# Two-layer diffusion trunk with a 32-expert layer: routed tokens moved by indirect DMA, experts ordered by count, plain float32 products

## The reference, cut to what matters

```python
def moe(h, lp):
    shp = h.shape
    t = h.reshape(-1, shp[-1])
    s = jax.nn.sigmoid((t @ lp['w_router']).astype(F32))
    _, idx = lax.top_k(s + lp['b_router'].astype(F32), TOP_K)
    s_sel = jnp.take_along_axis(s, idx, axis=-1)
    wts = s_sel / jnp.sum(s_sel, axis=-1, keepdims=True) * ROUTED_SCALE
    gates = jnp.sum(jax.nn.one_hot(idx, N_EXPERTS, dtype=F32) * wts[..., None], axis=1).astype(t.dtype)
    hid = jax.nn.silu(jnp.einsum('td,edf->tef', t, lp['w_exp1'])) * jnp.einsum('td,edf->tef', t, lp['w_exp3'])
    routed = jnp.einsum('tef,efd->td', hid * gates[:, :, None], lp['w_exp2'])
    shared = (jax.nn.silu(t @ lp['w_sh1']) * (t @ lp['w_sh3'])) @ lp['w_sh2']
    return (routed + shared).reshape(shp)
...
    h = rmsnorm(x, lp['g_norm2']) * (1 + sc2) + sh2
    x = x + g2 * moe(h, lp)
```

## Time and profile before

| | |
|---|---|
| three runs | 2008.7, 2008.95, 2011.85 us; median 2008.95 us |
| the profiled execution | 2008.79 us |
| its span, first to last instruction | 2007.3 us |
| around the span | 1.5 us |
| TensorE busy | 1676.0 us, 83% of the span |
| VectorE, ScalarE, GpSimd busy | 1128.2, 613.9, 677.4 us |
| moved by DMA | 315 MB, 157 GB/s over the span |

### The profile page before, as it was taken

How to read it: one execution, slowest core, us unless ns; L and a number is a source line. 1 busy time by engine, 2 the same in 40 slices (tenths; PEclk the granted TensorE clock), 3 DMA queues, 4 the chain that set the end, 5 groups by cost and what they waited for, 6 DMA issues and landing times. The chain is left out here.

```text
span 2007.3 us, 22880 instructions
## 1 busy us (share of the span) xinstructions
PE 1676.0 (83%) x7904; PEld 1209.8 (60%) x7904; DVE 1128.2 (56%) x1430; ACT 613.9 (31%) x1194; POOL 677.4 (34%) x293
## 2 busy tenths in 40 slices
PE   1344999988899999999985999978889999999994
PEld 0003445564777777777774444564777777777773
DVE  0112333373577777777775242372677777777775
ACT  0002122422243344333431112331443343334331
POOL 2202030031354454444543030030344454445442
PEclk9766999979899999999997899979989999999998
DMA  9994221202165565556651431110265565556551
GB/s 335 389 366 151 99 94 43 84 11 69 49 231 182 186 230 190 182 181 204 209 184 47 161 133 45 43 52 3 84 224 182 202 210 187 188 188 227 182 183 67
DMA packets 196679, 314.98 MB, mean 157 GB/s; under 512 B 18184, under 2 KB 153864, under 8 KB 193544
## 3 DMA queue, kind: packets, MB, share of 16 engines
q1 hardware_dynamic: 190792, 303.26, 43.9%
q0 software_dynamic: 5696, 10.77, 1.8%
q10 hardware_dynamic: 128, 0.13, 0.0%
HBM read 310.19 MB, written 5.94 MB: 157 GB/s over the span
## 5 line engine op out<-in xcount | busy, mean ns | idle before, releaser
L1547 POOL TENSOR_TENSOR low<-raw,high 128x2048 fp32r<-128x2048 f32 x64 | 421.3, 6583 | 522.8 <-DVE high L99 522.8
L1776 DVE TENSOR_TENSOR low<-raw,high 128x2048 fp32r<-128x2048 f32 x128 | 340.4, 2660 | 37.4 <-ACT high L1594 35.3
L749 PE MATMUL PS<-ringA,hT 128*128 128x512 f32 x672 | 302.8, 608 | 1.5 <-PE PS L749 0.6
L1664 PE MATMUL PS<-high,hTe 128*128 128x512 f32 x512 | 209.2, 409 | 69.1 <-POOL low L1547 64.2
L749 PEld LDWEIGHTS PS<-ringA,hT 128*128 128x128 f32 x672 | 128.2, 194 | 164.0 <-issue 161.6
L1665 PE MATMUL PS<-low,hTe 128*128 128x512 f32 x512 | 201.8, 394 | 0.0
L1666 PE MATMUL PS<-high,hTe 128*128 128x512 f32 x512 | 201.7, 394 | 0.0
L1580 ACT ACTIVATE hTe<-PS 128x512 fp32r<-128x512 f32 x256 | 153.4, 599 | 55.3 <-PE PS L1647 50.2
L99 DVE CAST high<-raw 128x2048 fp32r<-128x2048 f32 x128 | 156.3, 1221 | 17.4 <-DMA raw<-in_w_exp 16.6
L1722 PE MATMUL PS<-yh,PTb 128*128 128x512 f32 x384 | 153.7, 400 | 11.1 <-DVE acc L1809 11.1
L1664 PEld LDWEIGHTS PS<-high,hTe 128*128 128x128 f32 x512 | 96.6, 189 | 108.6 <-POOL low L1547 74.5
(11 more groups left out here) (292 smaller groups left out, 2645.8 us busy)
## 6 DMA issues: line engine op xcount, KB each, us to landing
raw<-in_w_exp SPq DMA_DIRECT2D x256, 512.0 KB, 4.8
raw<-in_w_exp SPq DMA_DIRECT2D x64, 1024.0 KB, 5.9
raw<-in_w_ada SPq DMA_DIRECT2D x24, 2048.0 KB, 26.8
ringA<-in_w_in SPq DMA_DIRECT2D x28, 1024.0 KB, 5.0
ringA<-in_w_out SPq DMA_DIRECT2D x8, 1024.0 KB, 4.9
ringB<-in_w_sh SPq DMA_DIRECT2D x8, 512.0 KB, 5.7
na_bias<-in_na_rpb POOLq DMA_DIRECT2D x32, 64.0 KB, 23.8
gate<-mod_rows POOLq DMA_DIRECT2D x4, 512.0 KB, 7.3
```

Of the source, the lines that this page charges most:

```text
L749: mm = pe.matmul(PS[:, u % 2, :], hT[:, k, t * P:(t + 1) * P], ring[:, s, c * 512:(c + 1) * 512], start=(k == 0), stop=(k == 7))
L1547: pool.tensor_tensor(hi(low[:, 1, :]), raw[:, 1, :], high[:, 1, :], ALU.subtract).then_inc(S["low_p"], 1)
L1664: pe.matmul(out, hi(ah), hi(wh), start=first, stop=False)
L1776: dve.tensor_tensor(hi(low[:, k, :]), raw[:, k, :], high[:, k, :], ALU.subtract).then_inc(S["low_v"], 1)
```

## The change

**Layout.** The host packs each expert's `w_exp1` and `w_exp3` beside each other, partition by partition, and `w_exp2` behind them: 16 KB and then 8 KB per partition in one row (`in_w_exp`, `in_w_sh`). One transfer brings up's weights (2 MiB), one brings down's (1 MiB).

**Units.** After the router the experts are ranked by count on the chip: experts 0 and 1 keep ranks 0 and 1 (their weights are loaded already in section B), the others follow by falling count. Ranks 0 to 9 get a unit of 128 slots each; the 22 other experts share 11 units, two experts of 64 slots side by side in column tiles (0, 0) and (0, 64). That makes 21 units, whole and paired ones alternating after the first two. A further pass over all units runs where a count exceeds its capacity.

```diff
+NS, NDF = 2, 8
+NF = NS + NDF
+NPAIR = (NE - NF) // 2
+NR13, NR2, NXG = 4, 5, 2
```

```diff
-                    norm_ev_dve(dve, 1, hT)
...
+                    dve.wait_ge(loaded, 64)
                     for t in range(T):
...
+                        dve.wait_ge(S["rstd_ready"], t + 1)
+                        v(dve.scalar_tensor_tensor(h2[:, t, :], x[:, t, :], rstd[:, t:t + 1], mrow[:, min(t, 1), 0, :], ALU.mult, ALU.mult))
+                        dve.tensor_tensor(h2[:, t, :], h2[:, t, :], mrow[:, min(t, 1), 1, :], ALU.add).then_inc(S["h2_ready"], 1)
```

```diff
+                    turn(0)
+                    pe.wait_ge(landed[3], 16)
+                    down(0)
+                    table(0)
+                    table(1)
                     turn(1)
+                    table(2).then_inc(S["table_mm"], 1)
+                    down(1)
                     turn(2)
                     down(2)
```

**Section C** is written out for the 21 units, with no cuts, no one-hot fetch and no one-hot return:

```diff
-                            pe.matmul(out, hi(ah), hi(wh), start=first, stop=False)
-                            pe.matmul(out, hi(ah), hi(wl), start=False, stop=False)
-                            return pe.matmul(out, hi(al), hi(wh), start=False, stop=last)
...
+                        for ranks in RANKS_OF[NS:]:
+                            expert = [sp.value_load(order[0:1, r:r + 1], min_val=0, max_val=NE - 1) for r in ranks]
+                            for r, e in zip(ranks, expert):
+                                i = place_of[r]
+                                if i >= NR13:
+                                    sp.wait_ge(S["w13_used"], i - NR13 + 1)
+                                sp.dma_start(ring13[:, i % NR13, :], A["w_exp"][l, e, :, W13]).then_inc(w13_in[i % NR13], 16)
...
+                                sp.dma_start(ring2[:, i % NR2, :], A["w_exp"][l, e, :, W2]).then_inc(w2_in[i % NR2], 16)
...
+                        def gather(u):
+                            b = u % NXG
+                            if u >= NXG:
+                                pool.wait_ge(xg_in[b], 16 * (u // NXG))
+                                pool.wait_ge(S["x_turned"], u - NXG + 1)
+                            pool.indirect_dma_start(xg[:, b, :], None, h2d[:, :], bass.IndirectOffsetOnAxis(ap=idx[:, 0, 0, u:u + 1], axis=0),
+                                                    bounds_check=T * P - 1, oob_is_err=False).then_inc(xg_in[b], 16)
...
+                        def scatter(u):
+                            b = u % 2
+                            if u >= 2:
+                                pool.wait_ge(y_out[b], 16 * (u // 2))
+                            pool.wait_ge(S["y_ready"], u + 1)
+                            pool.indirect_dma_start(yd[:, :], bass.IndirectOffsetOnAxis(ap=idx[:, 0, 1, u:u + 1], axis=0), y[:, b, :], None,
+                                                    bounds_check=T * P * TOPK - 1, oob_is_err=False).then_inc(y_out[b], 16)
...
+                        for u in range(NXG):
+                            gather(u)
+                        for u in range(NU):
+                            if u + NXG < NU:
+                                gather(u + NXG)
+                            scatter(u)
...
+                        def up(u):
+                            ranks = RANKS_OF[u]
...
+                            pe.wait_ge(S["xT_ready"], u + 1)
...
+                            for k in range(KC):
+                                for j, r in enumerate(ranks):
+                                    at, tile = columns(ranks, j)
+                                    mm = pe.matmul(PS[at, u % 2, :], xT[:, u % 2, k, at], w13_of(r, k),
+                                                   start=(k == 0), stop=(k == KC - 1), tile_position=tile)
+                            mm.then_inc(S["up_mm"], 1)
+                            if ranks[0] >= NS:
+                                pe.wait_ge(S["up_mm"], u + 1)
+                                pe.sem_inc(S["w13_used"], len(ranks))
...
+                        turn_in(0)
+                        for u in range(NU):
+                            up(u)
+                            if u + 1 < NU:
+                                turn_in(u + 1)
+                            if u:
+                                down(u - 1)
+                            turn(u)
+                        down(NU - 1)
...
+                        def keep(u):
+                            dve.wait_ge(S["down_mm"], u + 1)
...
+                            if u >= 2:
+                                dve.wait_ge(y_out[u % 2], 16 * (u // 2))
+                            dve.tensor_copy(y[:, u % 2, :].rearrange("p (b n) -> p b n", b=2), PS[:, 5:7, :]).then_inc(S["y_ready"], 1)
...
```

More of the change, by code:

```diff
@@ L45, with units @@
 NEG = -1e30
-SLOTS = P
-GROUP = 4
 SLOTF = 2048
 C_ID, C_IOTA, C_TRIU, C_ONES, C_TAB = 0, 128, 256, 384, 512
+NS, NDF = 2, 8
+NF = NS + NDF
+NPAIR = (NE - NF) // 2
+def units():
+    full, pairs = list(range(NS, NF)), [(NF + 2 * i, NF + 2 * i + 1) for i in range(NPAIR)]
+    out = [(r,) for r in range(NS)]
+    while full or pairs:
+        if pairs:
+            out.append(pairs.pop(0))
+        if full:
+            out.append((full.pop(0),))
+    return out
+RANKS_OF = units()
+NU = len(RANKS_OF)
+PASSES = 3
+RC_BROW, RC_BCOL, RC_IOTA, RC_DST, RC_LOOK = 0, 32, 33, 36, 48
+RC_N = RC_LOOK + 4 * P
+FIRST = 65536.0
+NONE = 4095.0
 T_MF, T_MB, T_COL, T_COS, T_SIN, T_LAM, T_SEL, T_N = 0, 128, 256, 320, 384, 448, 452, 964
@@ L88, in constants @@
         tab[h, T_SEL + h * P:T_SEL + (h + 1) * P] = 1.0
-    return c
-def hi(ap):
-    return ap.bitcast(F32R)
-def round_high(eng, out, in_):
-    return eng.tensor_copy(hi(out), in_)
+    rc = tab[:, T_N:]
+    e = np.arange(NE)
+    key = np.where(e < NS, FIRST * (NS - e), NE - 1 - e)
+    rc[:, RC_BROW:RC_BROW + NE] = key
+    rc[:NE, RC_BCOL] = key
+    rc[:, RC_IOTA] = p
+    for t in range(T):
+        for k in range(TOPK):
+            rc[:, RC_DST + t * TOPK + k] = NONE - (TOPK * (t * P + p) + k)
+    for u, ranks in enumerate(RANKS_OF):
+        cap = P // len(ranks)
+        for i, r in enumerate(ranks):
+            for q, val in enumerate((cap, 2 * cap, P * NU - cap, P * u + cap * i + 1)):
+                rc[r, RC_LOOK + q * P:RC_LOOK + (q + 1) * P] = val
+    return c
 class Chain:
@@ new lines, in router, with up @@
+                                return mm
+                            def up(t, half):
+                                for c in range(4):
+                                    k = 4 * half + c
+                                    mm = pe.matmul(PS[:, t, :], hT[:, k, t * P:(t + 1) * P], wsh[:, k * 512:(k + 1) * 512],
+                                                   start=(k == 0), stop=(k == KC - 1))
+                                if half:
+                                    mm.then_inc(S["sh_mm"], 1)
@@ L1366, in _ @@
+                            turn_in(0)
+                            turn_in(1)
+                            pe.wait_ge(landed[0], 16)
+                            router(0)
+                            turn_in(2)
+                            router(1)
+                            router(2).then_inc(S["rt_mm"], 1)
+                            pe.wait_ge(landed[2], 16)
+                            up(0, 0)
+                            up(0, 1)
                             pe.wait_ge(S["mask_ready"], 1)
+                            for w in range(T):
+                                pe.matmul(count, ones, mask[:, w, :], start=(w == 0), stop=(w == T - 1))
@@ L1367, in _ @@
+                            for w in range(T):
+                                pe.matmul(count_col, mask[:, w, :], ones[:, 0:1], start=(w == 0), stop=(w == T - 1))
                             for u in range(T):
@@ new lines, in _ @@
+                            v(dve.tensor_tensor(place, place, step_, ALU.add))
+                            v(dve.tensor_tensor(place, place, per_e(2), ALU.mult))
+                            v(dve.tensor_tensor(place, place, pos, ALU.add))
+                            v(dve.tensor_tensor(place, place, per_e(3), ALU.add))
+                            v(dve.tensor_tensor(place, place, mask, ALU.mult))
+                            for t in range(T):
+                                v(dve.max(r8[:, t, :], place[:, t, :]))
@@ L1627, in _, with take @@
[L1627 to L1634 removed]
+                                def take(u):
+                                    act.wait_ge(S["x_turned"], u + 1)
+                                    act.activation(xT[:, u % 2].rearrange("p (b c) n -> p b (c n)", b=2), PS[:, 2:4, :], ACT.Copy).then_inc(S["xT_ready"], 1)
@@ L1813, in _ @@
-                                one_hots(0, 0)
-                                one_hots(1, 2)
-                                for k in range(2):
-                                    cut_high(0, k, first=True)
-                                cut_low(0, 0)
-                                cut_low(0, 2)
-                                with dve.Fori(0, NG - 1) as g:
```

(3 more changed lines are left out.)

736 lines of the change are left out of this document (299 added, 437 removed).

## The result

The changed kernel takes 1927.36 us (median of 4 runs, 1919.92 to 1931.21), the kernel before took 2010.4 beside it (2008.7 to 2016.77). The ratio is 0.9577, with an interval of 0.9539 to 0.9615. The forecast was 1655 us, and 1927 lies well above its range.

The account below looks back on a forecast made before the run. TensorE's instruction count bounds the experts' section before the change, the fetch's wait after it. Per layer -211 (experts) + 17 (B) + 17 (D) = -177, twice -354: 2008.8 - 354 = 1655 us, range 1565 to 1780.

Parts of the forecast that it names:

- the landing: In the experts' section, an indirect fetch lands 7.0 us after its issue, with 2.0 and 14.8 as ends.
- The whole step: Per unit of experts: copy 1.2, two issues 2 x 1.0, landing 7.0, `turn_in` 1.0, `down` 3.5, together 14.7 us.
- section C: The experts: 323 us per layer against 534, 211 less.
- The clock is no rival of its own: TensorE in the experts' section: waits some 3 us; the clock held 0.99 after waits up to 1.9 us.
- its own formula: Experts' step: copy, two issues, landing, `turn_in` and `down` added up, 14.7 us with a landing of 7.0.
- The mechanism: GpSimd's queue: fetch(u+2) stands behind return(u-1), which waits for `y_ready`; TensorE waits some 3 us at `turn_in`; chance 0.50.
- A pair as one unit: TensorE in the experts' section: two experts side by side cost 1.0 units, with 2.0 (no overlap) as the other end.
- the slow rival: GpSimd writes the row list slowly: no gain at an issue of 5.9 us, 2187 us at 8.0; chance 0.04.
- One pass: Experts' units: counts fit one pass; rival, a second pass of an estimated 270 us, 1925 in all, chance 0.03.
- The rival in which the stream decides: Experts' section: fetch hidden, weights' stream sets 270 us, section 291 us, 1591 us in all; chance 0.28.
- B: The router's section: 72 us where it took 55, +17 us per layer, with +8 and +28 as ends.
- D: Section after the experts, three loads and sums: 27 us against 9, with one more barrier, +17 us per layer.

Follow-up runs that it names:

- experiment 3: Changed kernel with the fetch issued before the return, still behind `y_ready`, and the weights in DMAs of 4 KB per partition: 1677.73 us, ratio 0.8326.
- experiment 1: Changed kernel with each fetch issued two units earlier on GpSimd's queue, ahead of the return, still with two buffers: 1635.05 us, ratio 0.8128.
- experiment 5: Changed kernel with GpSimd's own loads held until the first `ringA` load lands, and VectorE doing GpSimd's sum after the experts: 1909.67 us, ratio 0.9514.

## Why the prediction was wrong, point by point

**The step that failed** is the landing: "I take 7.0, the nearest row". It was taken from 64 KB transfers beside the `w_ada` stream, but their first landing, 7.1 us, is the shortest of 32, of a transfer issued at 1.67 us, ahead of SP's first `w_ada` load (2.73). The first ones of the two later batches, at 56.31 and 111.27 us, with the stream running, landed after 9.2 and 8.3 us; the rest were set aside as a queue of their own making. Here the fetch too stands in a queue, behind the return's rows and beside weight descriptors that SP issues in the same microseconds, since the `up` and the `down` of a unit free the buffers for SP's next loads just as they lead to the fetch. Measured for two units from issue to landing: 9.5 + 15.0 us, where the forecast had twice 1.0 + 7.0.

**The whole step.** Two forecast steps are 29.4 us; two measured ones are 44.4. Of the 15.0 us between, the landing has 8.5. The way from the copy's start to the fetch's issue has 2.4 (770.10 to 773.49 is 3.4 us, not 2.2: some 0.85 us pass between the copy's end and the return's issue, 0.3 between the two issues). TensorE's lower clock behind the waits has 3.8 (`turn_in` and `down` together 12.8 us instead of 9.0). The rest, 0.3, is small gaps. That is 7.5 us per unit here; over all eighteen steps, 384 and 389 us instead of 265, it is 6.6 and 6.9, since the first step and the last few have little or no wait. These steps hold 119 and 124 of the 125 and 127 us that section C lacks; the way to the first down's end has 5 and 1.5 (37.8 and 34.5 us instead of 33), the rest 1.

**"The clock is no rival of its own"** fell with it: the waits were not 3 us but 6 to 11, and behind them the granted clock was 0.67 (763 to 770 us) and 0.75 (788.5 to 794.5). In experiment 3, with waits of some 2 us, it holds better: `turn_in` takes 1.09 us in the two units shown and the granted clock of C is 0.94, though six of the eighteen downs of layer 0 took 5.3.

**The range** was at fault beyond that. The prediction named 14.8 us as the landing's upper end and then let the range go only to 8.5. With the mean of the two units above, 12.2 us from the issue on, and nothing else changed, its own formula gives a step of 18.9 us, some 75 us more per layer and 1806 us in all; the clock and the gaps do the rest. An unknown price on the path of every step has to reach the range with its whole bound.

**What was right.** The mechanism, with a chance of 0.50: the order on GpSimd's queue puts the fetch behind `y_ready`, and TensorE waits at `turn_in` in nearly every unit. Experiment 1 shows it by undoing that part alone, experiment 3 by bringing the landing near its forecast size. A pair as one unit: up 7.09 us against 7.03, in experiment 1 down 3.65 against 3.60. The 9 us per layer that the prediction estimated for the changes of mode named by the Trainium skill's page "TensorEngine Tiling (Array Packing)", Key Properties, were too many. In experiment 1, where no fetch is waited for, the step from 643.42 with a pair's down and up takes 12.35 us, the next one with a whole unit's 11.89:

```profile
643.42 1.06 PE L1646 MATMUL PS<-cst,xg 128*128 128x128 f32 x8 [0.30 <-PE PS L1669]
...
655.77 1.06 PE L1646 MATMUL PS<-cst,xg 128*128 128x128 f32 x8 [0.32 <-PE PS L1669]
...
667.66 1.06 PE L1646 MATMUL PS<-cst,xg 128*128 128x128 f32 x8 [0.30 <-PE PS L1669]
```

That is 0.46 us per pair, some 5 us per layer, of which the longer records have 0.2; whether the rest is a change of mode no run shows. The issue took 1.01 us, not the 5.9 of the slow rival. One pass was enough: 42 fetches in two layers. The rival in which the stream decides, priced at 291 us for section C, is what experiment 1 brings about: 300.0 and 298.8.

**B** came out at +20 and +21 instead of +17. **D** at +22 and +21 instead of +17, of which GpSimd's sums are 2.6 and 2.3 (experiment 5); the three loads landed after 7.5, 12.0 and 16.5 us, where 7, 13 and 18 were forecast. **A** was not forecast: in layer 1 GpSimd issues its own ten loads from 1050.56 us on, 0.8 us ahead of SP's first `ringA` load, which then lands after 11.5 us; before, SP came first and the load landed in 3.8. The account closes on experiment 3, where C, B, D and A differ from their forecast by -5, +8, +9 and +12 us over both layers: 1655 and 24 are 1679, and its profiled execution took 1679.09.

## What to carry to other kernels

On an in-order queue that both fetches for the next step and returns the last one, put each fetch ahead of any return that can only begin after it would already be allowed; two buffers were enough for that here, and it was worth 292 us. Price a transfer that stands on the path by how it lands beside what will really stream next to it, and if only a bound is known, carry the bound into the range. When an engine waits on such a transfer, count its slower clock after the wait into the step.

## What was not expected of the hardware

- An indirect fetch of up to 128 rows took 4.2 us from issue to landing with no weights streaming, 7.4 beside 4 KB weight pieces with the return behind it, 9.5 or 15.0 beside 8 and 16 KB ones with the return ahead of it. Smaller descriptors in one queue shortened the landing in another, at the same bytes.
- A VectorE sum of two SBUF tensors took 3.25 us instead of 1.23 while GpSimd added, so the sums handed to GpSimd (2.9 to 3.4 us each) saved nothing: section D was 2.6 and 2.3 us shorter without them.
- Section B took some 74 us in most traces, but 67.4 in layer 1 of experiment 5, 67.0 in layer 0 of the kernel with the small pieces and the early fetch, 66.9 in layer 0 of that with the small pieces alone and 68.9 in layer 1 of that with the fetch first. Its first transposes came after a wait of 14 to 15 us at half speed in both of the cases below; in the long one the router's products and the start of the first `up` went on at half speed, in the short one the engine came up to full speed some 4 us after the wait. First the long case (layer 0 of the changed kernel), 16 router products and 16 matmuls of `up`:

```profile
502.41 3.46 PE L1354 MATMUL PS<-wr,hTB 128*128 128x32 f32 x16
...
514.11 9.24 PE L1361 MATMUL PS<-wsh,hTB 128*128 128x512 f32 x16
```

The same in the short case (layer 1 of experiment 5, lines one further):

```profile
1366.06 1.98 PE L1355 MATMUL PS<-wr,hTB 128*128 128x32 f32 x16
...
1372.28 7.11 PE L1362 MATMUL PS<-wsh,hTB 128*128 128x512 f32 x16
```

Nothing in section B differs between the two kernels; what decides which of the two happens stays open.
